# The first norm taken by token inside the gate unit's first tile, its low half split by two engines, x tiles 1 and 2 loaded alone, and a fourth convolution shift on VectorE

## The reference, cut to what matters

```python
D_MODEL, SEQ, CONV_KERNEL = 1024, 512, 31
def rmsnorm(x, g):
    return x * rsqrt(mean(x * x, axis=-1) + 1e-6) * g
def conformer_conv_module(h, ...):
    a = h @ w_pw1 + b_pw1                      # (512, 2048)
    u = a[..., :d] * sigmoid(a[..., d:])       # value * gate
    u = causal_dwconv(u, w_dw, b_dw)           # 31 taps, per channel
    u = silu(layernorm(u, ln_g, ln_b))
    return u @ w_pw2 + b_pw2
def reference(x, ...):                         # 2 layers
    x = x + conformer_conv_module(rmsnorm(x, norm_mix[0]), ...)
    x = x + conv_ffn(rmsnorm(x, norm_ffn[0]), ...)
    x = x + multiscale_pool_mixer(rmsnorm(x, norm_mix[1]), ...)
    x = x + conv_ffn(rmsnorm(x, norm_ffn[1]), ...)
    return rmsnorm(x, final_norm)
```

## Time and profile before

| | us |
|---|---|
| median of 3 runs | 950.68 |
| lowest, highest | 950.1, 1587.35 |
| the profiled execution | 950.07 |
| its span, first to last instruction | 948.3 |

### The profile page before, as it was taken

The page is one execution under the profiler, slowest core; times in us unless marked ns, Lnnn a source line. Parts: engine busy times, 40 slices in busy tenths (PEclk is TensorE's granted clock), DMA queues, the critical chain, the costliest instruction groups (busy, mean ns, idle before and its releaser), DMA issues.

```text
span 948.3 us, 11921 instructions
## 1 busy us (share of the span) xinstructions
PE 938.4 (99%) x4512; PEld 791.2 (83%) x4512; DVE 552.4 (58%) x703; ACT 393.4 (41%) x606; POOL 112.2 (12%) x74
## 2 busy tenths in 40 slices
PE   8999999999999999999999999999999999999997
PEld 6889899888888888888888898888888888888887
DVE  6899995657555555555434359765555655532333
ACT  7785596434333333332222355433333333322231
POOL 0558896000000000000000020000000000000000
PEclk9999999999999999999999999999999999999999
DMA  7320022233222222312232341233222232223212
GB/s 254 116 89 1 1 90 89 90 99 110 102 88 88 88 88 97 123 63 91 76 107 91 117 147 55 89 108 113 88 88 88 88 94 100 64 90 122 91 62 90
DMA packets 17020, 88.56 MB, mean 93 GB/s; under 512 B 2016, under 2 KB 4320, under 8 KB 9952
## 3 DMA queue, kind: packets, MB, share of 16 engines
q1 hardware_dynamic: 16416, 87.67, 27.2%
q10 hardware_dynamic: 576, 0.52, 0.2%
HBM read 86.09 MB, written 2.10 MB: 93 GB/s over the span
## 4 chain that ended last, share of the span: by engine, by line
PE 97%; DMA 1%; SPq 1%; DVE 0%; ACT 0%; issue 0%; DVEq 0%
PE bank L1138 29%; PE bank L1139 29%; PE bank L1140 29%; PE bank L1190 2%; PE bank L1191 2%; PE bank L1189 2%; DMA w_raw<-w_pw 1%; PE bank L1480 1%; PE bank L1224 1%; PE bank L1207 0%; PE bank L1448 0%; PE bank L1453 0%; PE bank L1452 0%; PE bank L1213 0%; PE bank L1342 0%; SPq L302 0%
## 5 line engine op out<-in xcount | busy, mean ns | idle before, releaser
L1138 PE MATMUL bank<-h_hi,w_hi 128*128 128x512 f32 x800 | 312.4, 390 | 1.4 <-DVE w_lo L768 1.4
L1140 PE MATMUL bank<-h_hi,w_lo 128*128 128x512 f32 x800 | 311.3, 389 | 0.0
L1139 PE MATMUL bank<-h_lo,w_hi 128*128 128x512 f32 x800 | 311.2, 389 | 0.0
L455 ACT ACTIVATE w_hi<-w_raw 128x2048 fp32r<-128x2048 f32 (+2 forms) x87 | 147.3, 1693 | 214.3 <-PE bank L1140 214.3
L768 DVE TENSOR_TENSOR w_lo<-w_raw,w_hi 128x2048 fp32r<-128x2048 f32 (+2 forms) x81 | 162.2, 2002 | 100.7 <-ACT w_hi L455 100.0
L1138 PEld LDWEIGHTS bank<-h_hi,w_hi 128*128 128x128 f32 x800 | 150.2, 188 | 33.5 <-DVE w_lo L768 1.8
L1139 PEld LDWEIGHTS bank<-h_lo,w_hi 128*128 128x128 f32 x800 | 150.2, 188 | 31.7 <-issue 0.5
L1140 PEld LDWEIGHTS bank<-h_hi,w_lo 128*128 128x128 f32 x800 | 150.2, 188 | 30.8
L1139 PE MATMUL bank<-u_lo,w_hi 128*128 128x512 f32 (+1 forms) x406 | 153.3, 378 | 0.0
L1138 PE MATMUL bank<-u_hi,w_hi 128*128 128x512 f32 (+1 forms) x374 | 141.0, 377 | 0.0
L1140 PE MATMUL bank<-u_hi,w_lo 128*128 128x512 f32 (+1 forms) x374 | 140.8, 377 | 0.0
(11 more groups left out here) (212 smaller groups left out, 1001.3 us busy)
## 6 DMA issues: line engine op xcount, KB each, us to landing
w_raw<-w_up SPq DMA_DIRECT2D x44, 1024.0 KB, 4.8
w_raw<-w_down SPq DMA_DIRECT2D x32, 704.0 KB, 4.0
w_raw<-w_pw SPq DMA_DIRECT2D x11, 1024.0 KB, 4.9
x_res<-x SPq DMA_DIRECT2D x3, 512.0 KB, 7.7
out<-out_sb SPq DMA_DIRECT2D x12, 128.0 KB, 1.9
w_raw<-w_pw SPq DMA_DIRECT2D x4, 256.0 KB, 7.7
w_raw<-w_pool SPq DMA_DIRECT2D x2, 512.0 KB, 3.7
band_raw<-band SPq DMA_DIRECT2D x1, 800.0 KB, 5.4
```

The lines of the kernel that those rows point to most:

```text
L455: nc.scalar.activation(w_hi[s][:, 0:columns], w_raw[s][:, 0:columns], ACT.Copy).then_inc(w_rounded[s], 1)
L1138: M.matmul(dst, a, hi, start=start, stop=False)
L1139: M.matmul(dst, a, lo, start=False, stop=False)
L1140: return M.matmul(dst, b, hi, start=False, stop=stop)
```

## The change

In the order of a run:

- SP's queue now holds parameters, part 0, x1, x3 with x4, x5 to x7, the gate unit, the tap parameters and the identity. ACT issues x0 first, and after its first table load x2, parts 1 and 2 in one transfer, and part 3.
- The small vectors for the pool mixer (`pool_shift`, `pool_gain`) are made on POOL at the start, not on DVE.
- The gate unit runs tile by tile (`second_unit`): the high passes of gate tile 0 need only ACT's rounding, then its low pass, then gate tile 1. DVE splits gate tile 0's weights (`first_lo`). POOL splits gate tile 1's, once `sumsq` is made, and then also the next value unit, which DVE split before.
- DVE adds the squares in pairs of tiles after its half of the split: four adds, and a fifth into `sumsq`. Its clearing of `sumsq` goes.
- The norm is taken by token: in the low pass of gate tile 0 four one-column matmuls make the sums with tokens on partitions, ACT takes the root of 128x4 values, DVE the reciprocal of 128x4, and during gate tile 1 four 128-column matmuls against the identity spread it over bank 5, from which ACT copies `rms`. ACT loads the root's table ahead and the sigmoid's after it.
- DVE drains, multiplies and starts the taps of tile 0 before those of tile 1. The hand-written places of scale, drain and multiply between the taps shift by 0 to 3 taps.
- `SHARED_SHIFTS` is 4: units 4 and 5 have 12 shifts, DVE 8 shared taps instead of 6, beginning 2 taps earlier.
- On ACT the tap columns (L514) come after the first sigmoids and the rounding of the next gate unit.

```diff
-SHARED_TILE, SHARED_SHIFTS = 6, 3
+SHARED_TILE, SHARED_SHIFTS = 6, 4
...
             sp.dma_start(par[:, 0:N_FIRST], vecs[:, 0:N_FIRST]).then_inc(par_loaded, 16)
-            load_x(0, 0, 1)
-            load_part(0)
+            load_parts(0, 0, 1)
             load_x(1, 1, 2)
-            load_x(2, 2, 4)
-            load_part(1)
-            load_x(3, 4, 6)
-            load_part(2)
-            load_part(3)
-            load_x(4, 6, 8)
+            load_x(3, 3, 5)
+            load_x(4, 5, 8)
...
-            pool.wait_ge(w_split[0], M_PW1 + 2)
+            pool.wait_ge(w_rounded[1], 1)
+            pool.wait_ge(first_lo, 1)
+            pool.wait_ge(summed, KD + 1)
+            nc.gpsimd.tensor_tensor(of_tile(w_lo[1], 1), of_tile(w_raw[1], 1), as_f32(of_tile(w_hi[1], 1)), SUB).then_inc(w_split[1], 1)
+            split(0, M_PW1 + 1)
+            split(1, M_PW1 + 1)
             pool.wait_ge(taps_rounded, 1)
...
+            load_x(0)
             act.wait_ge(consts_set, CONSTS)
-            nc.scalar.activation(warm[:, :], eps[:, 0:1], ACT.Copy)
+            nc.scalar.activation(warm[:, 0:1], eps[:, 0:1], ACT.Copy)
+            load_x(2)
+            load_parts(part_loaded[1], 1, 3)
+            load_parts(raw_loaded[0], 3, 4)
...
             round_unit(0, M_PW1 + 1, UNIT)
-            root(0)
...
+            touch_root()
+            act.wait_ge(stat_mm, 1)
+            nc.scalar.activation(root_tok[:, :], bank[BANK_SUM][:, 0:BLOCKS], ACT.Sqrt, scale=1.0 / D, bias=eps[:, 0:1]).then_inc(root_done, 1)
+            nc.scalar.activation(warm[:, 1:2], eps[:, 0:1], ACT.Sigmoid)
...
+            act.wait_ge(first_spread, 1)
+            nc.scalar.activation(rms[:, :], bank[BANK_FIRST][:, :], ACT.Copy).then_inc(first_read, 1)
+            first_sigmoid(0)
+            first_sigmoid(1)
+            round_unit(1, M_PW1 + 1, UNIT)
             tap_columns()
-            round_unit(1, M_PW1 + 1, UNIT)
-            sigmoid(0)
...
+            def add_squares(n):
+
+                dve.wait_ge(squared, Q_IN + 4 * n + 4)
+                V.tensor_tensor(in_sq[:, 4 * n:4 * n + 2, :], in_sq[:, 4 * n:4 * n + 2, :], in_sq[:, 4 * n + 2:4 * n + 4, :], ADD).then_inc(in_added, 1)
+                dve.wait_ge(in_added, 2 * n + 1)
+                V.tensor_tensor(in_sq[:, 4 * n, :], in_sq[:, 4 * n, :], in_sq[:, 4 * n + 1, :], ADD).then_inc(in_added, 1)
...
-            add_square(0)
-            add_square(1)
-            split_unit(1, M_PW1, UNIT)
-            for c in range(2, KD):
-                add_square(c)
-            split_unit(0, M_PW1 + 1, UNIT)
-            inverse(0)
+            dve.wait_ge(w_rounded[1], 1)
+            V.tensor_tensor(of_tile(w_lo[1], 0), of_tile(w_raw[1], 0), as_f32(of_tile(w_hi[1], 0)), SUB).then_inc(first_lo, 1)
+            add_squares(0)
+            add_squares(1)
+            dve.wait_ge(in_added, 4)
+            V.tensor_tensor(sumsq[:, :], in_sq[:, 0, :], in_sq[:, 4, :], ADD).then_inc(summed, KD + 1)
+            dve.wait_ge(root_done, 1)
+            V.reciprocal(root_tok[:, :], root_tok[:, :]).then_inc(rms_ready, 1)
...
+            dve.wait_ge(first_read, 1)
+            dve.wait_ge(first_gate, 1)
+            first_gate_drain(0)
             scale_val(0)
-            drain_gate(0)
-            multiply(0)
-            taps(0, 0, 8)
+            first_multiply(0)
+            tap(0, 0, 0)
+            tap(0, 0, 1)
+            dve.wait_ge(unit_done[1], 1)
+            first_gate_drain(1)
+            tap(0, 0, 2)
+            first_multiply(1)
+            for k in range(3):
+                tap(0, 1, k)
+            taps(0, 3, 7)
             scale_val(1)
-            taps(0, 8, 13)
+            taps(0, 7, 14)
             drain_gate(1)
-            taps(0, 13, 15)
+            taps(0, 14, 16)
             multiply(1)
...
-            taps(0, 26)
-            taps(1, 0, 8)
+            taps(0, 29)
+            taps(1, 0, 10)
             scale_val(3)
-            taps(1, 8, 15)
+            taps(1, 10, 17)
             drain_gate(3)
-            taps(1, 15, 16)
+            taps(1, 17, 18)
             multiply(3)
...
+            def second_unit():
...
+                pe.wait_ge(w_rounded[1], 1)
+                for k in range(KD):
+                    high(0, k)
+                pe.wait_ge(first_lo, 1)
+                for k in range(KD):
+                    if k == 4:
+                        pe.wait_ge(summed, KD + 1)
+                        sum_by_token(sumsq, start=True, stop=True).then_inc(stat_mm, 1)
+                    last = low(0, k)
+                last.then_inc(first_gate, 1)
+                for k in range(KD):
+                    if k == 1:
+                        pe.wait_ge(ident_loaded, 16)
+                        pe.wait_ge(rms_ready, 1)
+                        spread_blocks(bank[BANK_FIRST], root_tok, range(BLOCKS)).then_inc(first_spread, 1)
+                    high(1, k)
+                pe.wait_ge(w_split[1], 1)
+                for k in range(KD):
+                    last = low(1, k)
+                last.then_inc(unit_done[1], 1)
```

More of the change, by code:

```diff
@@ L283, in by_parity, with of_tile @@
             return ap[:, 0:2 * EVEN].rearrange("p (j q) -> p q j", q=2)
+        def of_tile(unit, t):
+            return unit[:, :].rearrange("p (k t c) -> p k t c", t=2, c=P)[:, :, t, :]
         def half_rows(half):
@@ L359, in _ @@
                 nc.gpsimd.memset(inv_count[:, t:t + 1], 1.0 / (t + 1)).then_inc(consts_set, 1)
+            pool.wait_ge(par_loaded, 16)
+            nc.gpsimd.tensor_tensor(pool_shift[:, :], col("pool_b", 0, KD), col("pool_s", 0, KD), MUL).then_inc(pool_vecs, 1)
+            for group, w in enumerate(WINDOWS):
+                nc.gpsimd.tensor_scalar(pool_gain[:, 2 * group:2 * group + 2], col("pool_s", 2 * group, 2), 1.0 / w, None, MUL).then_inc(pool_vecs, 1)
             def split(s, m):
@@ L383, in _ @@
             build(conv_lo, tap_lo, 0).then_inc(lo_built, 1)
-            split(1, M_PW1 + 1)
+            split(0, M_PW1 + 2)
             build(conv_lo, tap_lo, 1).then_inc(lo_built, 1)
-            split(0, M_PW1 + 2)
             split(1, M_PW1 + 2)
@@ L633, in _ @@
             nc.scalar.activation(bank[BANK_SQ_TOK][:, 0:T:P], bank[BANK_SQ_TOK][:, 0:T:P], ACT.Sqrt, scale=1.0 / D, bias=eps[:, 1:2]).then_inc(tok_root, 1)
-            nc.scalar.activation(warm[:, :], eps[:, 0:1], ACT.Silu)
+            nc.scalar.activation(warm[:, 0:1], eps[:, 0:1], ACT.Silu)
             def swish(c, tokens, n):
@@ L841, in _, with tap @@
             dve.wait_ge(ident_loaded, 16)
-            V.tensor_tensor(pool_shift[:, :], col("pool_b", 0, KD), col("pool_s", 0, KD), MUL).then_inc(pool_vecs, 1)
-            for group, w in enumerate(WINDOWS):
-                V.tensor_scalar(pool_gain[:, 2 * group:2 * group + 2], col("pool_s", 2 * group, 2), 1.0 / w, None, MUL).then_inc(pool_vecs, 1)
+            dve.wait_ge(pool_vecs, 1 + len(WINDOWS))
+            def tap(n, t, k):
+                c, acc = 2 * SUM_PAIRS[n] + t, bank[BANKS_ACC[t]][:, :]
+                src, w = glu[:, 2 * n + t, k:k + T], col("w_dw", c * TAPS + k)
+                if k:
+                    dve.wait_ge(tap_step[t], TAPS * n + k)
+                    V.scalar_tensor_tensor(acc if k < TAPS - 1 else conv_out[:, c, :], src, w, acc, MUL, ADD).then_inc(tap_step[t], 1)
+                else:
+                    dve.wait_ge(glu_done[t], SUM_PAIRS[n] + 1)
+                    if n:
+                        dve.wait_ge(tap_step[t], TAPS * n)
+                    V.tensor_scalar(acc, src, w, col("b_dw", c), MUL, ADD).then_inc(tap_step[t], 1)
             def taps(n, first=0, last=TAPS):
@@ L851, in taps @@
                     for t in range(2):
[L852 to L861 removed]
+                        tap(n, t, k)
             def scale_val(i):
@@ L1252, in first_unit, with high, low @@
                 last.then_inc(unit_done[0], 1)
-            def first_norm(k):
-                if k == 5:
-                    sum_channels(0)
+            def second_unit():
+                def high(t, k):
+                    a, dst = w_hi[1][:, (2 * k + t) * P:(2 * k + t + 1) * P], bank[BANKS_PW1[0][1] + t][:, :]
+                    M.matmul(dst, a, h_hi[:, k, :], start=k == 0, stop=False)
+                    M.matmul(dst, a, h_lo[:, k, :], start=False, stop=False)
+                def low(t, k):
+                    return M.matmul(bank[BANKS_PW1[0][1] + t][:, :], w_lo[1][:, (2 * k + t) * P:(2 * k + t + 1) * P], h_hi[:, k, :], start=False, stop=k == KD - 1)
+                pe.wait_ge(w_rounded[1], 1)
[18 more added lines that the diff above has]
+                last.then_inc(unit_done[1], 1)
             def second_norm(k):
@@ L1293, in wait_free @@
                     wait_drained((2, 3), DRAINED_PW1 + {(2, 0): 1, (3, 1): 3}[i, s])
-            for i in range(PW1_STEPS):
-                for s in range(0 if i else 1, 2):
+            second_unit()
+            for i in range(1, PW1_STEPS):
+                for s in range(2):
```

(2 more changed lines are left out.)

61 lines of the change are left out of this document (33 added, 28 removed).

## The result

Medians of 14 runs each: changed kernel 951.36 us (950.77 to 952.91), kernel before 949.92. The ratio over the runs (not exactly that of the medians) is 1.0018, 95% interval [1.0011, 1.0025]: 1.4 us longer, a small move but beyond its interval, where 0.4 us less was forecast. The profiled execution took 951.25 us (before: 950.07).

The account below looks back on a forecast made before the run. PE, busy 938.4 of 948.3 us, was taken to bound the kernel. From the profiled 950.07, 0.0 at the start and 0.4 less for the extra shift gave 949.7, plus 0.3 for scatter 950.0; range 948.8 to 952.1.

Parts of the forecast that it names:

- The landing of the pair, L = 10.4: Start: weight parts 1 and 2 land at 10.4 us, so tile 2 starts at 11.2 and the gain is 0.0.
- at most x3,4 and half of x5 to 7 go beside them: Start: other x transfers moving beside the pair make 2.54 MB, reached at 10.9 us; gives the latest landing, 12.5.
- the joined parts come late: Rival, start: the pair waits beside larger rows, landing at 11.2 to 12.5; total 950.8 to 952.1, centre 951.4; chance 0.25.
- plus 1.6: Start: lag in us added to 10.9, when the bytes are reached, for the pair's latest landing, 12.5.
- Each us costs one: Start: a later landing of the pair delays ACT's chain behind part 1 by as much, each us costing one.
- W: Gate unit: end of ACT's rounding of the gate weights, 18.54 us before, taken to hold.
- W + 5.95: Gate unit: DVE's last add for the sum of squares ends 5.95 us after W, at 24.5.
- The norm by token: Gate unit: sums and spreads cost PE 0.96 and 0.89 us, stall 0.5 at the sum; unit ends at 32.8, before 32.83.
- An earlier L would gain 0.5 at most: Start: if the pair and the gate weights land earlier, the weights by 0.5 at most, 0.5 us is gained.
- Hidden either way: Convolution: DVE's last add, ended at 141.09 and used by PE at 143.12 before, stays hidden despite DVE's shifts of about 1 us.
- The extra shift: Convolution: units 4 and 5 lose 0.71 us of matmuls, but unit 7 waits for ACT's drain: gain 0.37.
- The time outside the span: Whole kernel: time less span taken as 1.8 us, as in the profiled execution before.

Follow-up runs that it names:

- e4: Changed kernel with parts 1 and 2 as two transfers instead of one, still on ACT's queue: median 952.67 us.
- e5: Changed kernel with all early transfers on SP's one queue, x1, x2 and the parts single, nothing from ACT: median 950.74 us.
- e12: e7 with x tiles 5 and 6, part 3 and x7 as separate transfers, and the sum ahead of the second high step: median 948.53 us.
- e13: e7 with x tiles 5 and 6, part 3 and x7 as separate transfers, the sum left where e7 has it: median 948.69 us.
- e14: Kernel before with only four instead of three shared shifts: median 950.54 us.
- e7: e5 with sum ahead of the seventh low step, spread ahead of the third high one, and ACT's drain of units 4 and 5 moved earlier: median 949.78 us.
- e3: Changed kernel with three shared shifts instead of four: median 951.22 us.
- e11: e7 with three shared shifts instead of four: median 949.93 us.
- e2: Kernel before with only the changed kernel's list of transfers from two queues: median 951.07 us.
- e1: Changed kernel with the transfer list of the kernel before, one queue from SP: median 949.90 us.
- e9: e4 with the sum and the spread moved behind more matmuls, so that PE does not wait there: median 951.48 us.

## Why the prediction was wrong

**What bounds the kernel, and the accounting.** Right. PE's gaps before 34 us and at unit 7 hold the whole change of the span.

**The landing of the pair, L = 10.4: the step that failed.** I had bounds of 9.5 and 12.5 from the rates, and took 10.4 because the nearest row had part 1 there. That row came from a single queue, in which part 1 had only earlier things ahead of it. L was 11.8. The working had the term that decides, "at most x3,4 and half of x5 to 7 go beside them", and used it for the bound only. Before 10.4 could be taken it had to be said what would keep q1's larger rows behind q10's, and nothing would. The case that I called "the joined parts come late" is what happened: its chance was 0.25 and its centre 951.4. It named both halves of the mechanism; e4 and e5 size them, 0.64 for joining and 1.7 for the second queue and its order. That 951.36 falls on that centre is in part luck: by the sum, L = 11.8 gives +1.4 at the start, less 0.37, plus the 0.3 added for scatter; measured were +1.14, less 0.21, plus 0.25 outside the span. In the upper bound, "plus 1.6" has no row behind it, and the rate was higher than the 0.37 MB a us taken (425 GB/s from 8 to 11); neither decided the case. The Trainium skill, "DMA: Bandwidth & Descriptors", section "Queues, rings and completion order", says that a DMA engine takes turns between the queues with work, a packet at a time; the 203 and 197 packets agree. Whether a packet of the page is a packet of these records no run shows; the equal share holds either way.

**The price of a late L.** Nearly right. "Each us costs one": L is 1.4 later than taken, W 1.16 later (19.70 against 18.54), the rest having been slack before the gate weights. With 11.8 in place of 10.4, the step L + 0.77 gives tile 2 at 12.6 (12.62). W is 19.70, and W + 5.95 = 25.65 for the sum (25.66); 25.66 + 0.96 + 0.89 + 6.36 = 33.87 for the end (33.97).

**The norm by token.** Right: GpSimd's strided half 2.38 (2.3), its slack 33.97 - 32.72 = 1.25 (1.2), no stall at the spread. The short wait for sumsq was there, smaller than the 0.5 of the sum: PE comes to it 0.2 later than by the spacing of its matmuls (24.51 + 4 x 0.227 = 25.42 against 25.66).

**An earlier L would gain 0.5 at most.** Not by the landing of part 1 alone. e5 had part 1 at 9.5, but ACT then waited for the later x tiles, and the unit would have ended at 33.50 without the fall of the clock, 0.7 later than before. With the later tiles in order of need too, e12 and e13 end it at 32.41 and 32.05, 0.4 and 0.8 earlier than before. For the fall of the clock the prediction had no term: a stall at the sum was priced as a delay only, and in the profiled e5 it cost 1.7 more.

**DVE.** Right in the small: it waits 0.94 for scale_val(1), 1.22 for scale_val(3) and 1.00 for near_copied. DVE from 45 to 122 us in the changed kernel:

```profile
45.05 1.30 DVE L906 TENSOR_TENSOR bank<-bank,rms 128x512 f32<-128x512 f32 x2 [0.94 <-PE bank L1198]
...
100.07 1.30 DVE L906 TENSOR_TENSOR bank<-bank,rms 128x512 f32<-128x512 f32 x2 [1.22 <-PE bank L1198]
...
121.15 0.75 DVE L975 SCALAR_TENSOR_TENSOR bank<-glu_even,par,bank 128x512 f32<-128x512 f32 x1 [1.00 <-ACT sq L634]
```

"Hidden either way" was wrong as to its size: in e14 DVE ends `dev_sq` 1.2 later after the unit's end than in the changed kernel, and 0.55 is uncovered.

**The extra shift.** The mechanism was right, the term mis-sized: 0.21 of 0.71, not 0.37. From the last matmul of unit 6 (137.21) to the first of unit 7 (137.72) it is 0.51 where the spacing is 0.12, and the next comes 0.20 behind instead of 0.12: 0.47 of the 0.71 is lost there, against 0.34 in the prediction. That the drain is what holds it, e7, e12 and e13 show, with 0.67.

**The time outside the span** was taken as 1.8 and is 2.05. All kernels with both the new norm and four shifts have 2.05 (e12 2.0); three shifts (e3, e11), the new transfers alone (e2) and four shifts alone (e14) have 1.8. Its cause stays open.

## What to carry to other kernels

In this kernel a transfer given to a second queue did not come sooner, since the DMA engines were already full (DMA share 1.00 to 1.03): it shared them with everything on the first queue. So put what the busiest engine needs next into one queue, in order of need, in pieces as large as one use, and look at what the later pieces hold up. Before feeding PE earlier, look at what it will ask for next and whether that moves too; a wait of a microsecond in a busy stretch can cost more than its length (1.1 us cost 2.5 in e4's profile), and can be avoided by placing independent matmuls ahead of it. Where times fall into two groups, see which one the profile is of before explaining the median by it. For an operation moved onto a second engine, the slack is that of the last result in its chain, and a bank drained late by a third engine can hide the gain.

## What the runs showed of the hardware that I had not expected

- After PE had waited 1.1 us for the sum of squares, in a stretch otherwise full of matmuls, the granted clock was 0.66 (e4) and 0.57 (e5) from 27 to 31 us, that is mostly 1.2 GHz. After waits of 0.4 (e1), 0.7 (e7) and 0.3 us (e13) it stayed at 1.00 in the profiled runs. The two waits for tiles 1 and 2, 2.6 us together, left it at 1.00 in the changed kernel, but in e14 a wait of 2.3 us for tile 2 was followed by 0.77 from 10 to 15 us and 0.89 from 15 to 20:

```profile
PE bank L1241 <- ACT w_hi L485: 2.7, 2, 2.3
...
10.00:15.00 5.00, 3.38 (x10) 2.74 (x11) 3.97 (x7) 4.64 (x8) 0.00 (x0) 0.77 1.02 415
15.00:20.00 5.00, 5.00 (x21) 4.00 (x21) 4.17 (x6) 4.94 (x8) 0.00 (x0) 0.89 0.71 259
```

  Which waits are followed by a fall, these runs do not settle, and the same kernel need not show one each time. In the changed kernel 4 of 14 times lie at 952.5 to 952.9, 1.5 above the rest, with a mean granted clock of 0.997 to 0.998 against 0.998 to 0.999; e5 has 4 of 11 such times, e1 2 of 11. Among the 44 of e7, e9, e12 and e13 none lies 1.3 or more above its median. That these are the same fall was not seen in a trace.
- Two queues with work moved equal numbers of packets (203 and 197 in 4 us; 96 and 97 in its first half), so that the one with larger packets moved twice the bytes (1.15 and 0.56 MB).
- 0.25 us more outside the span, which appears only with two edits together.
